# A fused diffusion layer on one core: the later modulation rows are summed along rows on VectorE instead of down columns through TensorE

## What is computed

```
mod_x = jax.nn.silu(c) @ w_ada[l] + b_ada[l]
sh1, sc1, g1, sh2, sc2, g2 = jnp.split(mod_x[:, None, :], N_MOD, axis=-1)
h_x = _modulate(_rms_norm(x, norm1_gain[l]), sh1, sc1)
y_x, y_c = _token_mixer(h_x, h_c, w_in[l], four_w_out[l], ...)
x = x + g1 * y_x
h2 = _modulate(_rms_norm(x, norm2_gain[l]), sh2, sc2)
x = x + g2 * _sq_relu_mlp(h2, w_mlp1[l], w_mlp2[l])
return _rms_norm(x, final_gain)
```

## Time and profile before

| | |
|---|---|
| median of 3 runs | 1307.19 us (1306.77 to 1307.39) |
| profiled execution, first to last instruction | 1306.3 us |
| TensorE busy | 1278.7 us, 98% |
| VectorE busy | 875.5 us, 67% |
| ScalarE busy | 605.1 us, 46% |
| GpSimd busy | 147.0 us, 11% |
| mean granted clock of TensorE | 0.994 |

### The profile page before, as it was taken

One profiled execution on the slowest core, in us unless ns is written; L12 is line 12 of the kernel. 1 busy time (PEld: TensorE's weight loads), 2 busy tenths in 40 slices (PEclk: granted clock), 3 DMA queues, 4 the chain that ended last, 5 costly groups with the idle time before them and its releaser, 6 DMA issues.

```text
span 1306.3 us, 16741 instructions
## 1 busy us (share of the span) xinstructions
PE 1278.7 (98%) x6140; PEld 1044.1 (80%) x6140; DVE 875.5 (67%) x1397; ACT 605.1 (46%) x1039; POOL 147.0 (11%) x87
## 2 busy tenths in 40 slices
PE   5999999999999999999999999999999999999997
PEld 1788788888888778888788888888888888888886
DVE  3563577752556987768588766556646568868866
ACT  6871221242123544452668655545555433554444
POOL 0216330102231000014530000000000000000000
PEclk8999999999999999999999999999999999999999
DMA  9414220202256455567852544444438986468634
GB/s 382 154 33 146 81 97 1 65 13 66 65 191 219 146 193 202 182 252 278 297 185 73 191 155 161 137 149 162 151 114 281 316 281 222 162 215 266 192 100 162
DMA packets 95098, 220.09 MB, mean 168 GB/s; under 512 B 12436, under 2 KB 12692, under 8 KB 93992
## 3 DMA queue, kind: packets, MB, share of 16 engines
q1 hardware_dynamic: 83184, 189.58, 42.8%
q10 hardware_dynamic: 10040, 23.15, 4.9%
q0 software_dynamic: 1792, 6.29, 1.4%
HBM read 167.59 MB, written 51.40 MB: 168 GB/s over the span
## 4 chain that ended last, share of the span: by engine, by line
PE 93%; DVE 3%; DMA 2%; issue 1%; ACT 1%; POOL 0%; SPq 0%; ACTq 0%; DVEq 0%
PE ps L2726 16%; PE ps L2728 15%; PE ps L2727 15%; PE ps L3266 8%; PE ps L3274 8%; PE ps L3269 8%; PE ps L3109 4%; PE ps L3104 4%; PE ps L3106 4%; PE ps L3292 3%; PE ps L2804 2%; DMA ada_in<-in_w_ada 2%; PE ps L2930 1%; PE ps L2912 1%; PE ps L2871 1%
## 5 line engine op out<-in xcount | busy, mean ns | idle before, releaser
L1005 POOL TENSOR_TENSOR ring_lo<-raw,ring_hi 128x1024 fp32r<-128x1024 f32 x42 | 102.7, 2458 | 500.4 <-ACT ring_hi L1088 500.3
L2726 PE MATMUL ps<-t_hi,s_hi 128*128 128x512 f32 x392 | 153.1, 391 | 0.0
L2728 PE MATMUL ps<-t_hi,s_lo 128*128 128x512 f32 x392 | 153.1, 391 | 0.0
L2727 PE MATMUL ps<-t_lo,s_hi 128*128 128x512 f32 x392 | 153.1, 390 | 0.0
L1646 ACT ACTIVATE s_hi<-s_raw 128x512 fp32r<-128x512 f32 x112 | 70.5, 630 | 115.2 <-DMA b<-in_w_stream 58.1
L2605 DVE TENSOR_TENSOR s_lo<-s_raw,s_hi 128x512 fp32r<-128x512 f32 x112 | 77.3, 690 | 44.5 <-ACT s_hi L1646 44.0
L2726 PE MATMUL ps<-ring_hi,hT_hi 128*128 128x512 f32 x232 | 94.2, 406 | 0.0
L2728 PE MATMUL ps<-ring_hi,hT_lo 128*128 128x512 f32 x232 | 90.7, 391 | 0.0
L2727 PE MATMUL ps<-ring_lo,hT_hi 128*128 128x512 f32 x232 | 90.5, 390 | 0.0
L2726 PEld LDWEIGHTS ps<-t_hi,s_hi 128*128 128x128 f32 x392 | 73.6, 188 | 16.2 <-DVE t_lo L2609 0.4
L2727 PEld LDWEIGHTS ps<-t_lo,s_hi 128*128 128x128 f32 x392 | 73.6, 188 | 15.9
(11 more groups left out here) (474 smaller groups left out, 3151.6 us busy)
## 6 DMA issues: line engine op xcount, KB each, us to landing
s_raw<-ff_scr SPq DMA_DIRECT2D x112, 256.0 KB, 2.9
raw<-in_w_stream SPq DMA_DIRECT2D x34, 512.0 KB, 4.3
ff_scr<-ffs SPq DMA_DIRECT2D x16, 1024.0 KB, 4.8
t_raw<-in_w_stream SPq DMA_DIRECT2D x64, 256.0 KB, 3.5
w_B_raw<-in_w_stream SPq DMA_DIRECT2D x48, 256.0 KB, 2.8
ff_scr<-ffa SPq DMA_DIRECT2D x16, 768.0 KB, 4.5
b<-in_w_stream SPq DMA_DIRECT2D x48, 256.0 KB, 4.3
ada_in<-in_w_ada SPq DMA_DIRECT2D x8, 1024.0 KB, 14.9
```

Of the source, the lines that this page charges most:

```text
L1005: nc.gpsimd.tensor_tensor(lo_ap, raw_of(i), hi_ap.bitcast(F32), ALU.subtract).then_inc(split, 1)
L2726: M(dst, lhsT=l_hi, rhs=r_hi, start=first, stop=False, skip_group_check=goes_on)
L2727: M(dst, lhsT=l_hi, rhs=r_lo, start=False, stop=False, skip_group_check=goes_on)
L2728: return M(dst, lhsT=l_lo, rhs=r_hi, start=False, stop=last, skip_group_check=goes_on)
```

## The change

- The pieces of `w_ada` for the four later rows are now laid out transposed on the host (`ada_columns`: piece `jj` holds 128 modulation channels as partitions, and the 1024 inputs along the row). They are as large as before, 512 KB each. The first two rows' part of `w_ada` is a tensor of its own.
- `add_row(jj)` is now one `tensor_tensor_reduce`: it multiplies the piece with a row of `silu(c)`, which stands in all partitions alike, sums along the row, and writes 128 finished modulation values to one column of `gate_cols` (rows 0 and 3) or `mod2` (rows 1 and 2). It no longer depends on the piece before.
- The row of `silu(c)` is made by a store of 1024 single values to DRAM (`silu_scr`, in ScalarE's loop at j = 12) and a load that spreads them over the partitions (`silu_row`, behind `copy_heads(0)`). From piece 16 on a copy of it in PSUM is read, made by one `tensor_copy`.
- `reduce_row` on TensorE and `row_out` on ScalarE are gone, the two loads into `mod2` and VectorE's wait for them too. Two stores of 1024 single values (`store_gate`) bring the gate rows to DRAM, from where `g1b` and `g2b` are loaded as before.
- `add_row(8)` moves behind `g_add("22", 2)`; it stood ahead of it.
- The waits on the old semaphores become waits on `mod_done`.

```diff
-            eng.dma_start(ada_place(j)[:], ins["w_ada"][(j % 8) * P:(j % 8 + 1) * P, (2 + j // 8) * D:(3 + j // 8) * D]
-                          ).then_inc(ada_landed(j)[0], 16)
+            eng.dma_start(ada_place(j)[:], ins["ada_columns"][j]).then_inc(ada_landed(j)[0], 16)
...
+                    with nc.allow_non_contiguous_dma(reason="1024 values of c, one per row"):
+                        act.dma_start(silu_scr[0].rearrange("(c p) -> p c", p=P), silu_c[:, :, 0]).then_inc(silu_stored, 16)
...
-            def row_out(a, banks):
-
-                for half in range(2):
-                    act.wait_ge(ada_red, 2 * a + half + 1)
-                    if a:
-                        act.wait_ge(row_stored, 32 * a)
-                    row = ada_row[32 * half:32 * half + 1, :]
-                    A(row, ps[32 * half:32 * half + 1, banks + half, :], ACT.Copy).then_inc(ada_row_out, 1)
-                    act.wait_ge(ada_row_out, 2 * a + half + 1)
-                    act.dma_start(mod_scr[a:a + 1, half * 512:(half + 1) * 512], row).then_inc(row_stored, 16)
+            def store_gate(a):
+
+                act.wait_ge(mod_done, (8, 32)[a])
+                with nc.allow_non_contiguous_dma(reason="1024 modulation values, one per row"):
+                    act.dma_start(gate_scr[a].rearrange("(c p) -> p c", p=P), gate_cols[:, a, :]).then_inc(gate_stored, 16)
...
             copy_heads(0)
+            act.wait_ge(ab_ready, 7)
+            act.wait_ge(silu_stored, 16)
+            act.dma_start(silu_row[:], silu_scr[0:1, :].to_broadcast([P, D])).then_inc(silu_in, 16)
             hi_to(("fo", 1))
...
-                if j == 2:
-                    row_out(0, 2)
+                if j == 3:
+                    store_gate(0)
...
             load_ada(act, 28)
-            row_out(2, 0)
             hi_to(("wo", 10))
             load_ada(act, 29)
-            act.wait_ge(row_stored, 16 * 6)
-            with nc.allow_non_contiguous_dma(reason="2048 modulation values, one per row"):
-                for a in range(2):
-                    act.dma_start(mod2[:, a, :], mod_scr[1 + a, :].rearrange("(c p) -> p c", p=P)).then_inc(gates_in, 16)
...
             z_norm(3)
-            row_out(3, 0)
+            store_gate(1)
...
             def add_row(jj):
-                kt = jj % 8
-                src = ada_place(jj)
-                late = jj >= 16
-                total = ps[:, 2:4, :].rearrange("p a b -> p (a b)") if late else ada_acc[:]
-                dve.wait_ge(*ada_landed(jj))
-                if kt == 7 and late or kt == 0 and 0 < jj < 16:
-                    dve.wait_ge(ada_red, 2 * (jj // 8))
-                if jj == 16:
-                    dve.wait_ge(ada_row_out, 4)
-                if kt == 0:
-                    do.chain(V.tensor_scalar(total, src[:], silu_c[:, 0, 0:1], None, ALU.mult), ada_acc_done)
-                else:
-                    do.chain(V.scalar_tensor_tensor(ada_acc[:] if kt == 7 else total, src[:], silu_c[:, kt, 0:1], total,
-                                                    ALU.mult, ALU.add), ada_acc_done)
+                a, c = jj // 8, jj % 8
+                src = ada_place(jj)
+                total = gate_cols[:, a // 3, c:c + 1] if a in (0, 3) else mod2[:, a - 1, c:c + 1]
+                if jj == 0:
+                    dve.wait_ge(silu_in, 16)
+                dve.wait_ge(*ada_landed(jj))
+                row = ps[:, 2:4, :].rearrange("p a b -> p (a b)") if jj >= 16 else silu_row[:]
+                if jj == 16:
+                    do.chain(V.tensor_copy(row, silu_row[:]))
+                do.chain(V.tensor_tensor_reduce(src[:], src[:], row, 1.0, 0.0, ALU.mult, ALU.add, total), mod_done)
...
+                if j == 2:
+                    add_row(8)
                 g_los(j + 1, LATER_UNITS[2:])
...
                 g_add("11", j + 1)
-                add_row(6 + 2 * j)
+                if j > 1:
+                    add_row(6 + 2 * j)
...
-            dve.wait_ge(gates_in, 16 * 2)
             do.chain(V.tensor_tensor(mod2[:], mod2[:], bmod2[:], ALU.add))
...
-            def reduce_row(a, bank):
-                pe.wait_ge(ada_acc_done, 8 * (a + 1))
...
-                for half in range(2):
-                    M(ps[32 * half:32 * half + 1, bank + half, :], lhsT=ones[:],
-                      rhs=ada_acc[:, half * 512:(half + 1) * 512],
-                      start=True, stop=True).then_inc(ada_red, 1)
...
                 gate_product(p, m)
-                if (p, m) in ((5, 2), (2, 6)):
-                    reduce_row(m // 6, 2)
...
-                        if (step, kp, t) in ((1, 3, 0), (2, 2, 3)):
-                            reduce_row(step + 1, 0)
```

More of the change, by code:

```diff
@@ L279, in program @@
         hss = small("hss", [P, 3, NT, HEADS])
+        gate_cols = small("gate_cols", [P, 2, KT])
         cols = small("cols", [P, 2, 2])
@@ L318, in program @@
         b_sb = place("b_sb", o_t, [P, HALF])
-        ada_acc = place("ada_acc", o_t + 2048, [P, D])
-        ada_row = place("ada_row", o_t + 6144, [64, 512])
+        silu_row = place("silu_row", o_t + 2048, [P, D])
         yr_first = [place("yr_first0", o_kv + 12288, [P, SEQ]), place("yr_first1", o_t + 16384, [P, SEQ])]
@@ L374, in program @@
         wpm_scr = nc.dram_tensor("wpm_scr", [KT, P, 512], F32, kind="Internal").ap()
-        mod_scr = nc.dram_tensor("mod_scr", [4, D], F32, kind="Internal").ap()
+        gate_scr = nc.dram_tensor("gate_scr", [2, D], F32, kind="Internal").ap()
+        silu_scr = nc.dram_tensor("silu_scr", [1, D], F32, kind="Internal").ap()
         raw_in = [sem("raw_in0"), sem("raw_in1")]
@@ L446, in program @@
         ada_raw_in = sem("ada_raw_in")
[L447 to L450, removed]
+        mod_done = sem("mod_done")
+        silu_stored = sem("silu_stored")
+        silu_in = sem("silu_in")
+        gate_stored = sem("gate_stored")
         acc_in = [sem(f"acc_in{i}") for i in range(4)]
@@ L534, in load_ada @@
             elif j < 18:
-                eng.wait_ge(ada_acc_done, j)
+                eng.wait_ge(mod_done, j)
             elif j < 21:
@@ L538, in load_ada @@
             else:
-                eng.wait_ge(ada_acc_done, {29: 27, 30: 28, 31: 30}.get(j, j - 3))
+                eng.wait_ge(mod_done, {29: 27, 30: 28, 31: 30}.get(j, j - 3))
             if j == 4:
                 eng.wait_ge(merge_done, ret_count(KT - 1, 1))
-            eng.dma_start(ada_place(j)[:], ins["w_ada"][(j % 8) * P:(j % 8 + 1) * P, (2 + j // 8) * D:(3 + j // 8) * D]
-                          ).then_inc(ada_landed(j)[0], 16)
+            eng.dma_start(ada_place(j)[:], ins["ada_columns"][j]).then_inc(ada_landed(j)[0], 16)
         def gate_wait(eng, p, m):
@@ L964, in _ @@
                 if s == 2 * FP + 1:
-                    sp.wait_ge(row_stored, 16 * 8)
-                    sp.dma_start(g2b[:], mod_scr[3:4, :].to_broadcast([P, D])).then_inc(gates_in, 16)
+                    sp.wait_ge(gate_stored, 16 * 2)
+                    sp.dma_start(g2b[:], gate_scr[1:2, :].to_broadcast([P, D])).then_inc(gates_in, 16)
                     sp.dma_start(b2b[:], ins["b_ada"][:, 5 * D:6 * D].to_broadcast([P, D])).then_inc(gates_in, 16)
@@ L1342, in g_copy @@
                     else:
-                        act.wait_ge(ada_acc_done, 4)
+                        act.wait_ge(mod_done, 4)
                 A(dst[:], ps[:, b, :], ACT.Copy).then_inc(up_copied, 1)
@@ L1464, in _ @@
             act.wait_ge(y_ready, KT - 1)
-            act.dma_start(g1b[:], mod_scr[0:1, :].to_broadcast([P, D])).then_inc(gate1_in, 16)
+            act.wait_ge(gate_stored, 16)
+            act.dma_start(g1b[:], gate_scr[0:1, :].to_broadcast([P, D])).then_inc(gate1_in, 16)
             act.dma_start(b1b[:], ins["b_ada"][:, 2 * D:3 * D].to_broadcast([P, D])).then_inc(gate1_in, 16)
@@ L1587, in _ @@
             z_square(6)
-            act.wait_ge(row_stored, 16 * 8)
+            act.wait_ge(mod_done, 32)
             z_modulate_pair(0, (1, 3))
@@ L2678, in _ @@
                 if s == 2 * FP + 4:
-                    dve.wait_ge(gates_in, 16 * 5)
+                    dve.wait_ge(gates_in, 16 * 3)
                     do.chain(V.tensor_tensor(g2b[:], g2b[:], b2b[:], ALU.add), g_ready)
@@ L3114, in _ @@
                 gate_product(p, m)
-                if (p, m) in ((5, 2), (2, 6)):
-                    reduce_row(m // 6, 2)
             def z_transposes(c):
                 if c == 0:
-                    pe.wait_ge(ada_acc_done, 32)
+                    pe.wait_ge(mod_done, 32)
                 pe.wait_ge(xhat, 10 + 4)
@@ L3415, in layouts @@
         "cc": np.stack([a["c"][0], a["c_ctx"]], -1).reshape(KT, P, 2).transpose(1, 0, 2),
-        "w_ada": a["w_ada"][0], "b_ada": b_ada,
+        "w_ada": a["w_ada"][0][:, :2 * D], "b_ada": b_ada,
+        "ada_columns": a["w_ada"][0][:, 2 * D:].T.reshape(32, P, D),
         "bmod1": col(b_ada[0, :2 * D]),
```

10 lines of the change are left out of this document (removed).

## The result

| | before | changed |
|---|---|---|
| median, 22 runs each | 1307.41 us | 1310.11 us |
| lowest to highest | 1305.91 to 1309.50 | 1306.10 to 1315.59 |
| ratio (95% interval) | 1 | 1.0021 (1.0013 to 1.0030) |
| profiled execution, first to last instruction | 1306.3 us | 1312.3 us |
| TensorE busy | 1278.7 us | 1278.0 us |

1303.9 us was forecast. The change is slower by 2.7 us, between 1.7 and 3.9, and it spreads more from run to run than the kernel before. The profiled execution is one of the long ones (1314.1 us), so its waits are at the large end; why the cost differs so much from run to run stays open.

A forecast was written before the change was run, and what follows sets the result against it. From 50 us on TensorE's products were taken to bound the time. The terms -4.6 - 0.1 + 0.8 + 0.0 + 0.6 gave -3.3 us, from 1307.2 to 1303.9; 8-in-10 range 1302.2 to 1306.0.

The forecast's parts named there:

- Transfers: Three new stores of 1024 single values, two such loads gone: none on the path; without cover each costs 4 to 7 us.
- Reductions: Four reduce_row product groups leave TensorE's list, from 483 us on: 1.15 us each, 4.6 us gained in all.
- The price of the sum along a row: VectorE's new multiply-and-sum over 1024 columns takes 1.27 us start to next start, 0.05 less than before; bounds 1.2 and 1.5.
- slower: half rate: Rival: VectorE's sums with two fp32 SBUF sources run at half rate, 1.2 us more each; +3.9, 1311 us; chance 0.05.
- Piece 8 and the first gain: At product (3, 2) TensorE waits 0.8 us for VectorE's release, losing most of the first 1.15 us; moving piece 8 gains nothing.
- The last chunk: In the norm stage, weight chunk 15 lands late for ScalarE's rounding, so TensorE waits 0.6 us; bounds 0 and 1.4.
- The second gain, (1, 7): At the remainders of (1, 7), slack of 1.2 us covers the reduction's 1.15: no wait, upper bound 0.4 us.
- The copy into PSUM: VectorE's copy of the silu(c) row ahead of piece 16 takes 1.3 us, hidden by 1.28 us of waiting: 0 on path.
- full gain: Rival: piece 7's load and the last chunk come soon enough, TensorE waits nowhere anew: -4.7, 1302.5 us; chance 0.12.
- Nothing comes of it: Rival: the reductions' products on TensorE overlap those around them and cost nothing, so nothing is gained; chance 0.02.
- norm stage: Rival: behind 650 us load-bound chains let TensorE keep only 1.6 to 2.4 us: 1304.8 to 1305.6 us; chance 0.17.

The follow-up runs named there:

- before_plus_store: The kernel before plus one store of 1024 neighbouring single values, read by nobody, behind the fourth z_norm: 1314.17 us, ratio to before 1.0050.
- dense_store: The changed kernel with gate channels permuted on the host, so each gate store writes 128 pieces of 32 bytes: 1303.44 us, ratio to before 0.9965.
- dense_piece8_first: dense_store with add_row(8) put back ahead of g_add("22", 2): 1303.89 us, ratio to before 0.9969.
- dense_both: dense_store with the third store, of silu(c) at 277 us, also made in pieces of 32 bytes: 1303.07 us, ratio to before 0.9962.

## Why the prediction was wrong, point by point

- **The step that failed: "Transfers".** It priced the three stores by their own landing ("without that cover each would cost its 4 to 7 us"), from the rows of two loads of the same shape, and looked only for who reads what they write. A load of 1024 single values took 4.0 us; a store took 12.2 and 18.4, and while it ran the core moved 14 and 108 GB/s. What counted was who else had a transfer under way: in the norm stage chunk 15 took 13.8 us for 6.8, and TensorE waited 8.0 us for it. The one in the norm stage costs 6.7 us by itself (before_plus_store), the changed kernel's two together 6.7 (against dense_store). Sum: 1303.4 + 6.7 = 1310.1. No rival held this; the one on the other side was about VectorE.
- **Reductions, -4.6.** Right: (7, 2) follows (5, 2) with no gap, and the doubled ones cost 0.86 us each for the second pair. From the last remainders of (5, 2) to product (3, 2) it took 7.53 us before (481.90 to 489.43) and takes 6.35 in dense_store (481.19 to 487.54): this reduction is gained whole.
- **The price of the sum along a row, 1.27 us.** Right, to 0.01 us: 1.22 for the sum and 0.08 for its result, next start 1.27 us later (476.75 to 478.02):

```profile
476.75 1.22 DVE L2137 CUSTOM_DVE_ANT_0 ada_next<-ada_next,silu_row 128x1024 f32<-128x1024 f32 x1 [0.87 <-DMA ada_next<-in_ada_columns]
477.90 0.08 DVE L2137 DVE_READ_ACCUMULATOR2_ANT gate_cols<- 128x1 f32 x1
478.02 1.23 DVE L2230 TENSOR_TENSOR yf_in<-yf_in,sig_a 128x1024 f32<-128x1024 f32 x1
```

  The rival "slower: half rate" falls: 31 of the 32 sums take 1.22 or 1.23 us, 15 of them with both operands in SBUF (the other one is piece 1, below). The rule of the Trainium skill (Vector Engine (DVE) Microarchitecture Reference, Points that are easy to get wrong) doesn't show here. The page states it for the form `S2S2D2_STT`; whether this instruction has that form no run shows. The old instruction of the earlier trace rows, with two fp32 operands in SBUF as well but no sum along the row, took 1.29 us.
- **Piece 8 and the first gain, +0.8.** Mis-sized: no wait in dense_store, 0.27 us in the changed kernel. Two parts came sooner than taken. Piece 7 landed in 3.4 to 3.5 us for 3.9 (the prediction's "a few tenths faster"); with its rows apart the wait is 0.7 us. And moving piece 8, which the prediction put at nothing since "the copy ends the wait as before", gives 0.4 us (above). It went by the releaser that the row of `sig_b` names, but in the trace of before ScalarE's copy was done at 488.16, 0.48 us ahead of the start of `sig_b`:

```profile
487.56 0.60 ACT L1344 ACTIVATE g_uw<-ps 128x512 f32<-128x512 f32 x1 [1.14 <-DVE sig_a L2229]
```

  From the start of piece 8 to that of `sig_b` it took 1.26 us there, and 1.27 with the sum in its place (dense_piece8_first, 485.89 to 487.15). So the old piece 8 cost the chain no less than the sum, and not its busy time of 0.74.
- **The last chunk, +0.6.** The chain was the right one (chunk 15, its rounding, `z_modulate(5)`, the third pair of transposes), and the 8 us came through it. Without the two gate stores of single values it isn't late at all: chunk 15 is issued at 641.71 in dense_store, 6.0 us sooner than before, where the prediction had 2.4. (TensorE is 0.7 us ahead in that trace before the first reduction, which leaves 5.3; what brought the loads forward so far was not taken apart.) ScalarE's chain is not held back by the loads: `z_norm(3)` ends 6.0 us sooner as well (644.25 for 650.21), while TensorE's first transposes come 5.4 us sooner (646.76 for 652.19).
- **The second gain, (1, 7): 0.** Right within its bound of 0.4: 0.2 us in the changed kernel, none in dense_store.
- **The copy into PSUM, 1.3 us, hidden.** Right: 1.22 us, with nobody behind it.
- **The rivals.** What the change is worth without the hold-up is near the "full gain", with TensorE waiting nowhere anew: 1302.5 forecast, 1303.4 and 1303.1 measured. "Nothing comes of it" falls with the doubled reductions. The forecast of 1303.9 lies close to these two by luck in part: the waits that it counted, +0.8 and +0.6, aren't there, and less than its 4.6 us came off the time all the same (4.0 in dense_store). With rows 16 KB apart the time is that of the "norm stage" case: 1305.5, for 1304.8 to 1305.6.

## What to carry to other kernels

A store that writes single values from many partitions side by side in DRAM is to be priced by what it does to the transfers around it and not by its own landing: lay the data out so that a partition writes 32 bytes or more in one piece, or put the store where no load is waited for within some 15 us (an estimate, from stores that took 12 to 19 us here). Of pieces shorter than 32 bytes only pairs of values were tried, and they still cost 2.2 us. The host's layout can pay for this, as a permutation of the columns did here. When a change brings a kind of transfer that the trace lacks in that direction, a row of the other direction (a load for a store) is no bound of its price.

## What was not expected of the hardware

- The hold-up has about the same size for 128, 512 and 1024 neighbouring single values (6.7 to 6.9 us of time), and isn't seen for 128 pieces of 32 bytes or for values 512 bytes apart. The Trainium skill (DMA: Bandwidth & Descriptors, Specifications) gives 512 bytes as the smallest piece at full rate, with read-modify-write below it. The runs agree that small pieces are slow for themselves (12.7 us for 4 KB). But the rule goes by length alone, and values 512 bytes apart are as short as neighbours and don't hold up the others.
- A load of the same 1024 single values does nothing of the kind: the two were issued at 633.3 and 633.7 us, and the two weight chunks issued at 634.9 and 638.1 landed in 4.2 and 5.2 us.
- One sum along a row, piece 1, took 3.07 us:

```profile
393.89 3.07 DVE L2137 CUSTOM_DVE_ANT_0 ada_first<-ada_first,silu_row 128x1024 f32<-128x1024 f32 x1
```

  GpSimd had begun a subtraction with two SBUF operands 0.40 us ahead of it:

```profile
393.49 2.39 POOL L1005 TENSOR_TENSOR ring_lo<-raw,ring_hi 128x1024 fp32r<-128x1024 f32 x1 [2.73 <-ACT ring_hi L1088]
```

  The sum ends 1.08 us after that one's end. In the trace of before VectorE began first (395.20 for 395.57), and there its sum took 1.28 us and GpSimd's subtraction 3.18. In dense_store and dense_both GpSimd is first again, and the sum takes 3.17 and 2.83 us. The later of the two seems to wait for the earlier; no run tested it, and nothing waited for this sum.
- After TensorE had stood still for 8 us, its products ran at 1.2 GHz (0.43 us from start to start). From the third pair of transposes to the fourth it takes 12.03 us (652.72 to 664.75), in dense_store 2.25 (651.28 to 653.53); less the wait of 7.98 us, 1.8 us are left, which I put down to the clock.
